# First block of a two-block kernel: another order for the convolution, TensorE's small products, the norm scaling and the rotations

## What is computed

```python
def hybrid_mixer(h, positions, w_in, ...):
    z, xbc, dt_raw, q, k, v, g_ssd, g_att = split_columns(h @ w_in)      # 1024 x 7440
    y_ssd = ssd_mixer(z, xbc, dt_raw, ...) @ w_ssd_out
    q = rope(q, positions); k = rope(k, positions)
    y_att = moba_attention(q, k, v) @ w_attn_out       # 16 heads of 64, causal
    merged = sigmoid(g_ssd) * y_ssd + sigmoid(g_att) * y_att
    return merged @ w_out

def ssd_mixer(z, xbc, dt_raw, ...):
    xbc = silu(causal_dwconv(xbc, conv_w, conv_b))     # 4 taps, 1280 channels
    dt = softplus(dt_raw + dt_bias)                    # 16 heads
    # per chunk of 128 tokens: decay sums of dt*A, decay matrix exp(difference),
    # y_diag = (C B^T * decay) X dt, states, y_off = C states * decay
    y = (y_diag + y_off + X * d_skip) * silu(z)
    return rms_norm per group of 512 columns (y) * norm_w
```

## Time and profile before

| | us |
|---|---|
| three runs | 1402.92, 1403.53, 1398.72 |
| median | 1402.92 |
| span of the profiled execution (the page gives no other time for it) | 1396.5 |
| PE busy | 1319.0 (94%) |
| DVE busy | 841.3 (60%) |
| ACT busy | 727.8 (52%) |
| POOL busy | 600.3 (43%) |

### The profile page before, as it was taken

How to read it: one execution, slowest core, us unless ns; L and a number is a source line. 1 busy time by engine, 2 the same in 40 slices (tenths; PEclk the granted TensorE clock), 3 DMA queues, 4 the chain that set the end, 5 groups by cost and what they waited for, 6 DMA issues and landing times. The chain is left out here.

```text
span 1396.5 us, 22606 instructions
## 1 busy us (share of the span) xinstructions
PE 1319.0 (94%) x7927; PEld 1064.2 (76%) x7927; DVE 841.3 (60%) x1458; ACT 727.8 (52%) x1234; POOL 600.3 (43%) x316
## 2 busy tenths in 40 slices
PE   7989997998899999999889998989999998999997
PEld 6877886776787787878667776767888886788885
DVE  1392436546789888888368899964777763211112
ACT  5555556446476666666564344555433433544443
POOL 5959667440000000000488476836100016687875
PEclk9989998799899999999999999899999999999999
DMA  6736532138599999997475465623100005455562
GB/s 219 204 105 196 154 119 91 61 123 267 177 331 339 322 323 325 328 309 263 143 207 161 135 167 165 187 88 121 62 3 2 17 25 171 153 172 189 170 190 91
DMA packets 128507, 239.97 MB, mean 172 GB/s; under 512 B 16428, under 2 KB 33710, under 8 KB 128420
## 3 DMA queue, kind: packets, MB, share of 16 engines
q1 hardware_dynamic: 116656, 227.12, 51.2%
q10 hardware_dynamic: 11765, 11.67, 3.0%
HBM read 234.57 MB, written 1.05 MB: 169 GB/s over the span
## 5 line engine op out<-in xcount | busy, mean ns | idle before, releaser
L301 POOL TENSOR_TENSOR wlo<-raw,whi 128x1024 fp32r<-128x1024 f32 (+1 forms) x224 | 554.5, 2499 | 623.3 <-ACT whi L296 618.8
L296 ACT ACTIVATE whi<-raw 128x1024 fp32r<-128x1024 f32 (+1 forms) x300 | 308.9, 1053 | 219.9 <-PE bank L325 150.3
L321 PE MATMUL bank<-whi,t0h 128*128 128x512 f32 (+1 forms) x584 | 243.8, 418 | 8.3 <-ACT whi L296 5.7
L322 PE MATMUL bank<-whi,t0l 128*128 128x512 f32 (+1 forms) x584 | 237.2, 406 | 0.0
L325 PE MATMUL bank<-wlo,t0h 128*128 128x512 f32 (+1 forms) x584 | 160.5, 397 | 0.3 <-POOL wlo L301 0.3
L321 PEld LDWEIGHTS bank<-whi,t0h 128*128 128x128 f32 x584 | 115.2, 197 | 41.8 <-ACT whi L296 6.9
L322 PEld LDWEIGHTS bank<-whi,t0l 128*128 128x128 f32 x584 | 115.0, 197 | 25.8 <-issue 1.2
L325 PEld LDWEIGHTS bank<-wlo,t0h 128*128 128x128 f32 x584 | 112.1, 192 | 26.4 <-POOL wlo L301 0.8
L301 DVE TENSOR_TENSOR wlo<-work,whi 128x1024 fp32r<-128x1024 f32 x96 | 113.0, 1219 | 7.8 <-ACT whi L296 7.8
L1605 PE MATMUL bank<-whi,t0h 128*128 128x512 f32 x256 | 106.5, 416 | 0.5 <-issue 0.5
L1606 PE MATMUL bank<-whi,t0l 128*128 128x512 f32 x256 | 101.7, 397 | 0.0
(11 more groups left out here) (521 smaller groups left out, 2486.7 us busy)
## 6 DMA issues: line engine op xcount, KB each, us to landing
raw<-in_w_ff SPq DMA_DIRECT2D x64, 512.0 KB, 3.7
raw<-in_w_in SPq DMA_DIRECT2D x60, 496.0 KB, 3.8
raw<-in_w_in SPq DMA_DIRECT2D x56, 512.0 KB, 3.8
work<-in_w_exp_down SPq DMA_DIRECT2D x68, 256.0 KB, 6.1
work<-in_w_exp_gate SPq DMA_DIRECT2D x62, 256.0 KB, 5.7
work<-in_w_exp_up SPq DMA_DIRECT2D x62, 256.0 KB, 7.4
raw<-in_w_exp_down SPq DMA_DIRECT2D x60, 256.0 KB, 5.9
raw<-in_w_exp_gate SPq DMA_DIRECT2D x34, 256.0 KB, 5.8
```

The source lines that it names most:

```text
L296: nc.scalar.activation(whi[:, s, 0:width], raw_of(n)[:, 0:width], ACT.Copy).then_inc(hi_ready, 1)
L301: ins = (nc.vector if split_by_vector(n) else nc.gpsimd).tensor_tensor(wlo[:, s, 0:width], raw_of(n)[:, 0:width], whi[:, s, 0:width].bitca ...
L321: nc.tensor.matmul(dst[t][:, 0:width], hi[:, k, r], wh[:, kk, :], start=k == 0 and not begun, stop=False)
L322: nc.tensor.matmul(dst[t][:, 0:width], lo[:, k, r], wh[:, kk, :], start=False, stop=False)
```

## The change

- The convolution's sums of the first three taps lie in PSUM (banks 4 to 7, two chunks of 256 columns in each), in groups of eight and two chunks; the fourth tap writes SBUF. It stands behind the first five steps of `dt` instead of ahead of them. `pe_sums_of_decay` waits for the whole convolution, since it writes bank 6.
- PE's table `within` puts the mixer's products behind quarters of a tile instead of behind tiles, and most of them some tiles earlier; ACT's table follows. `pe_sums(q)` comes behind the second quarter of tile 7+q, `pe_diagonal(q)` behind the third of tile 8+q.
- `dve_angles` stands between `xdt_ready` and the wait for `state_done`. The start of y (`begin_y`) stands behind the first `differences`.
- The four norm steps go from DVE to ACT (`act_normed`). y is transposed within tile 14 and split into buffers of its own, `yh` and `yl`.
- `rot` and `rtmp` are doubled. Rotation 1 waits for the last eviction alone, rotation i for the transposes of i-2. POOL's loop is written out; rotation 0 has a semaphore of its own.

```diff
-        y_mean, y_root = sem("y_mean"), sem("y_root")
-        turn_y = Turn(y, gain("ssd_norm_w"), t0h, t0l)
+        y_mean, y_root, y_inverse = sem("y_mean"), sem("y_root"), sem("y_inverse")
+        yh, yl = rounded_over(work_at, "yh", 7680, KC, SEQ), rounded_over(work_at, "yl", 9728, KC, SEQ)
+        turn_y = Turn(y, gain("ssd_norm_w"), yh, yl)
...
-        rot = [carve(2304 + 512 * x, 2, NT, P) for x in range(2)]
-        rtmp = [carve(3328 + 128 * x, NT, 2, 32) for x in range(2)]
+        rot = [[carve(at + 512 * x, 2, NT, P) for x in range(2)] for at in (2304, 11776)]
+        rtmp = [[carve(at + 128 * x, NT, 2, 32) for x in range(2)] for at in (3328, 12800)]
...
-
-
-            between = {3: [pe_xbc], 6: [pe_sums_of_decay, pe_x_back], 7: [pe_cb], 8: [pe_state], 9: [pe_off]}
+                    for part in within.get((p, q), ()):
+                        part(pe)
+                    if q == 1 and SUMS_AT <= p < SUMS_AT + 4:
+                        pe_sums(pe, p - SUMS_AT)
+                    if q == 2 and SUMS_AT < p <= SUMS_AT + 4:
+                        pe_diagonal(pe, p - SUMS_AT - 1)
+
+            within = {(3, 1): [pe_xbc], (5, 2): [pe_sums_of_decay], (5, 3): [pe_x_back], (6, 2): [pe_cb], (7, 0): [pe_state],
+                      (7, 1): [pe_off], (14, 0): [pe_turn_y_first], (14, 1): [pe_turn_y_second]}
             for p in range(IN_T):
                 tile(p)
-                for part in between.get(p, ()):
-                    part(pe)
-                if 9 <= p < 13:
-                    pe_sums(pe, p - 9)
-                if 10 <= p < 14:
-                    pe_diagonal(pe, p - 10)
-            turn_y.pe(pe, [(y_normed, 4)])
             pe.wait_ge(evac_in, NT * IN_T)
...
+        SUMS_AT = 7
+
+        def pe_turn_y_first(pe):
+            turn_y.pe(pe, [(y_normed, 2)], (0, 1))
+
+        def pe_turn_y_second(pe):
+            turn_y.pe(pe, [(y_normed, 4)], (2, 3))
...
-            wide_quarter(pe, Q_SSD + j, j % 4, bank[0:2], t0h, t0l)
+            wide_quarter(pe, Q_SSD + j, j % 4, bank[0:2], yh, yl)
...
-            between = {3: [act_dt_exp], 5: [act_dt_ln, act_conv_silu], 6: [act_z], 7: [act_decays], 8: [act_angles], 13: [act_squares]}
+            between = {2: [act_dt_exp], 3: [act_dt_ln], 4: [act_z, act_conv_silu], 5: [act_decays], 11: [act_angles],
+                       12: [act_squares], 13: [act_normed]}
...
-                if 9 <= p - 1 < 13:
-                    act_lmat(act, p - 10)
+                if SUMS_AT <= p - 1 < SUMS_AT + 4:
+                    act_lmat(act, p - 1 - SUMS_AT)
...
-            pe.wait_ge(xbc_copied, XCH // 2)
+            pe.wait_ge(conv_done, XCH)
...
-            for w in range(4):
...
-                    if w == 0:
-                        order.mark(nc.vector.tensor_scalar(convT[:, c, :], xbcT[:, c, 0:SEQ], tap, None, ALU.mult))
...
-                        ins = nc.vector.scalar_tensor_tensor(out=convT[:, c, :], in0=xbcT[:, c, w:w + SEQ], scalar=tap,
-                                                             in1=convT[:, c, :], op0=ALU.mult, op1=ALU.add)
...
-                order.settle()
             dve.wait_ge(dt_exp, 2)
             order.step(nc.vector.tensor_scalar(s_u, s_exp, 1.0, None, ALU.add))
...
+
+            def partial1(c):
+
+                return bank[4 + c % 8 // 2][:, (c % 2) * SEQ:(c % 2) * SEQ + SEQ]
+
+            for chunks in (range(8), range(8, XCH)):
+                for w in range(4):
+                    for c in chunks:
+                        tap = cwT[:, w * XCH + c:w * XCH + c + 1]
+                        if w == 0:
+                            order.mark(nc.vector.tensor_scalar(partial1(c), xbcT[:, c, 0:SEQ], tap, None, ALU.mult))
+                        else:
+                            ins = nc.vector.scalar_tensor_tensor(out=convT[:, c, :] if w == 3 else partial1(c),
+                                                                 in0=xbcT[:, c, w:w + SEQ], scalar=tap,
+                                                                 in1=partial1(c), op0=ALU.mult, op1=ALU.add)
+                            if w < 3:
+                                order.mark(ins)
+                            else:
+                                ins.then_inc(conv_done, 1)
+                    if w < 3:
+                        order.settle()
+                dve.wait_ge(conv_done, chunks.stop)
...
-            dve_angles(dve, order)
             dve.wait_ge(cum_done, 1)
...
             nc.vector.tensor_tensor(xdtd.rearrange("p (e d) -> p e d", d=DH),
                                     xdt[:, 0, :].rearrange("p (e d) -> p e d", d=DH),
                                     edec.unsqueeze(2).to_broadcast([P, NH, DH]), ALU.mult).then_inc(xdt_ready, 1)
+            dve_angles(dve, order)
             dve.wait_ge(state_done, 1)
             nc.vector.tensor_copy(prevT, bank[7][:, :]).then_inc(state_ready, 1)
-            for t in range(NT):
-                order.mark(nc.vector.tensor_tensor(y[:, t, :].rearrange("p (e d) -> p e d", d=DH),
...
-            order.step(nc.vector.tensor_tensor(y[:, 1, :], y[:, 1, :], xdtd, ALU.add))
+
+            def begin_y():
+
+                for t in range(NT):
+                    order.mark(nc.vector.tensor_tensor(y[:, t, :].rearrange("p (e d) -> p e d", d=DH),
+                                                       xs[:, t, :].rearrange("p (e d) -> p e d", d=DH),
+                                                       dsk.unsqueeze(2).to_broadcast([P, NH, DH]), ALU.mult))
+                dve.wait_ge(off_done, 1)
...
@@ -931,6 +952,8 @@
                 differences(q)
                 if q:
                     add_diagonal(q - 1)
+                else:
+                    begin_y()
...
-            order.step(nc.vector.reciprocal(stat[:, 0:4], stat[:, 0:4]))
-            for t in range(NT):
-                for g in range(2):
-                    o = y[:, t, 512 * g:512 * g + 512]
-                    nc.vector.tensor_scalar(o, o, stat[:, 2 * t + g:2 * t + g + 1], None, ALU.mult).then_inc(y_normed, 1)
+            nc.vector.reciprocal(stat[:, 0:4], stat[:, 0:4]).then_inc(y_inverse, 1)
             turn_y.dve(dve)
-            rotate(dve, nc.vector, order, 0)
+            rotate(dve, nc.vector, order, 0, rot_first, 0)
...
+        def act_normed(act):
+            act.wait_ge(y_inverse, 1)
+            for g in range(2):
+                for t in range(NT):
+                    o = y[:, t, 512 * g:512 * g + 512]
+                    nc.scalar.activation(o, o, ACT.Copy, scale=stat[:, 2 * t + g:2 * t + g + 1]).then_inc(y_normed, 1)
+            turn_y.act(act, 0)
+
         def act_after_in(act):
-            turn_y.act(act, Q_SSD)
...
-        def rotate(eng, ops, order, i):
-
-            if isinstance(i, int) and i == 0:
+        def rotate(eng, ops, order, i, ready, before):
+
+            if i < 2:
                 eng.wait_ge(sin_done, 2)
                 eng.wait_ge(evac_in, NT * IN_T)
+            else:
+                eng.wait_ge(qk_turned, 2 * (i - 1))
...
-            if not (isinstance(i, int) and i == 0):
-                eng.wait_ge(qk_turned, 2 * i)
+            tmp = rtmp[min(i, 1)]
...
-                    dst = rot[x][:, a].rearrange("p t (h a d) -> p t h a d", h=2, a=2)
+                    dst = rot[i % 2][x][:, a].rearrange("p t (h a d) -> p t h a d", h=2, a=2)
...
-                last.then_inc(rot_ready, 1)
-                eng.wait_ge(rot_ready, 2 * i + x + 1)
+                last.then_inc(ready, 1)
+                eng.wait_ge(ready, before + x + 1)
 
         def pool_rotations(pool):
             order = Order(pool, pool_order)
-            with pool.Fori(0, PAIRS // 2 - 1) as i:
-                order.body(0, i, ATT_POOL)
-                rotate(pool, nc.gpsimd, order, i + 1)
-            order.after(0, PAIRS // 2 - 1, ATT_POOL)
+            for i in range(1, PAIRS // 2):
+                rotate(pool, nc.gpsimd, order, i, rot_ready, 2 * (i - 1))
...
-                    pe.wait_ge(rot_ready, 2 * i + x + 1)
+                    if i:
+                        pe.wait_ge(rot_ready, 2 * (i - 1) + x + 1)
+                    else:
+                        pe.wait_ge(rot_first, x + 1)
```

More of the change, by code:

```diff
@@ L843, in dve_ssd @@
             dve.wait_ge(taps_ready, 2)
-            for w in range(4):
-                for c in range(XCH):
-                    tap = cwT[:, w * XCH + c:w * XCH + c + 1]
-                    if w == 0:
-                        order.mark(nc.vector.tensor_scalar(convT[:, c, :], xbcT[:, c, 0:SEQ], tap, None, ALU.mult))
-                    else:
-                        ins = nc.vector.scalar_tensor_tensor(out=convT[:, c, :], in0=xbcT[:, c, w:w + SEQ], scalar=tap,
-                                                             in1=convT[:, c, :], op0=ALU.mult, op1=ALU.add)
-                        if w < 3:
-                            order.mark(ins)
-                        else:
-                            ins.then_inc(conv_done, 1)
```

(1 more changed line is left out.)

30 lines of the change are left out of this document (13 added, 17 removed).

## The result

| | before | changed |
|---|---|---|
| median of 20 runs, us | 1404.42 | 1394.93 |
| lowest, highest | 1397.35, 1409.07 | 1389.34, 1406.19 |
| span of the profiled execution | 1396.5 | 1391.1 |

The ratio is 0.9947 with an interval of 0.9933 to 0.9962: the changed kernel is faster by 5 to 9 us. A second set gave 1398.33 (12 runs) against 1401.34 (23), ratio 0.9971 (0.9946 to 0.9996), 1 to 8 us. The forecast was 1408, slower by 5.

A forecast was written before the change was run, and what follows sets the result against it. TensorE was taken to bound the first block, through five holes and the half clock behind them. Terms 3.4 (up to tile 14) + 9.2 (to the scores) - 7.3 (attention) = +5.3 us on 1402.9 gave 1408, range 1390 to 1420.

The forecast's parts named there:

- The term for attention: Scores to turn of output: GpSimd waits and half clock go, some clock loss returns; 3.5 + 4.6 + 1.6 - 2.4 = -7.3 us.
- the slow stretch around it begins before that hole, so I leave it: Attention, around rotation 3: only the 1.56 us wait for GpSimd goes; the slow clock around it stays.
- the 2.4: Attention's step 0: starting behind a long wait at half clock gives back about half of the 4.6 us won, 2.4.
- 23 x (0.41 + 0.21) = 14.3: Rotation 0 after tile 14: VectorE gets one step per GpSimd step of rotation 1, 14.3 us for 23 steps.
- signs of being wrong: `pe_off` without a wait, rotation 0 under 8 us, or scores under 18 us after tile 14; then time under 1400.
- +9.2: Tile 14 to scores, with turn of y and its wait: 22.4 + 1.9 + 0.6 - 15.7 = +9.2 us.
- the wait for `dA`: Tile 5, after its third quarter: PE waits 2.7 us (0 to 4.5) for `dA`, plus 1.7 of clock (0 to 3.4).
- The wait for `prevT`: Tile 7: angle steps held by GpSimd's subtractions delay `prevT`; PE waits 5.4 us (0 to 8), plus 2.7 of clock.
- the rival of the gaps: Angle steps slip into GpSimd's gaps while rotations alternate; the wait and its clock (8.1 us) go: 1400 us, chance 0.20.
- the one in which VectorE keeps its turns: GpSimd can't get between VectorE's steps, so angles and rotation 0 cost what they do now: -18.6, 1384 us, chance 0.20.
- The third rival, the clock staying down: Half clock lasts longer behind three new waits, through attention's first step: +14, 1417 us, chance 0.26.
- Small products between quarters: 0: Moving `pe_sums` and `pe_diagonal` to other places costs and gains nothing, 0 us.

The follow-up runs named there:

- run with rotation 3 late: Changed kernel in which rotation 3 alone waits for the turn of rotation 2, as before the change; 1398.27 us against 1402.46 before, ratio 0.9980.
- run with GpSimd behind VectorE: Changed kernel, but GpSimd starts rotation 1 only when VectorE has finished rotation 0; 1401.36 us against 1402.46 before, ratio 0.9986.
- two buffers alone: Kernel before with the rotations double-buffered and nothing else; 1391.20 us against 1401.39 before, ratio 0.9929.
- the convolution alone: Kernel before with the convolution's sums in PSUM, in its old place, and nothing else; 1394.92 us against 1401.39 before, ratio 0.9951.
- the run with the angles later: Changed kernel with the 14 angle steps moved in front of the last add_diagonal, the sines one tile later; 1390.13 us against 1402.46 before, ratio 0.9909.
- version with rotation 0 early: Changed kernel with angles later and rotation 0 in VectorE's idle stretches under tiles 12 to 14; 1386.39 against 1401.39 us before, again 1385.60 against 1401.34.

## Why the forecast was wrong

**What failed first: the second slow stretch.** The term for attention was -7.3 and measured -13.9 (-13.4 in the second profile). The step that failed is "the slow stretch around it begins before that hole, so I leave it". By steps: 0 and 1 together became 7.6 us shorter where 5.7 were forecast (3.5 + 4.6 - 2.4; the half clock behind the first scores lasted until 232.7 only, so the 2.4 was nearer 1.2), step 2 became 5.6 shorter where 1.6 was, step 3 0.7 where 0 was: 1.9 + 4.0 + 0.7 = 6.6. The run with rotation 3 late brings 4.8 of step 2's 5.6 us back. The forecast read rightly that the clock fell before the hole, and took from it that the stretch had another cause and would stay. It hung on the late rotation all the same: none of the nine profiles without a late rotation 3 shows the stretch. What joins the late rotation to a fall ahead of its own wait is not shown.

**Second: the price of two alternating streams.** "23 x (0.41 + 0.21) = 14.3" had the right mechanism and the wrong size. It added the time from start to start of each engine working alone; beside each other a pair takes 0.48, and in the changed kernel VectorE got in a step more now and then, 22 steps from 219.84 to 229.23, 0.43 each (first and last here). That makes 9.4 instead of 14.3, 4.9 of the 5.6 us. The rest of that term was right: VectorE's rotation began 2.4 us after tile 14 (forecast 2.3), GpSimd's subtractions ended 6.2 us after it (forecast 6.9). One of the forecast's own signs of being wrong came true by this: scores less than 18 us after tile 14 (16.8), with a time under 1400; and rotation 0 took 13.3 us (215.91 to 229.23), not over 15.

```profile
219.84 0.55 DVE L1082 TENSOR_TENSOR work<-proj,work 128x128 f32<-128x128 f32 x1
...
228.95 0.28 DVE L1085 TENSOR_TENSOR work<-work 128x128 f32<-128x128 f32 x1
```

**Third: two terms that were one.** The sum set "+9.2" for the sharing against "-7.3" for the double buffer, each with bounds of its own. The run with GpSimd behind VectorE shows that they are one trade: what rotation 0 won there (4.7 us), steps 0 and 1 lost to rotation 1 and the clock behind it (5.2).

**What was right.** The part up to the first decay sums: the wait for `dA` was 2.70 (forecast 2.7), the transposes ahead of the convolution came at 52.36 (52.4), the convolution ended at 81 (81.0), its steps took 0.48 to 0.49 us each as recorded, in 16.6 us (forecast 17; before, 31). The clock behind the wait for `dA` cost 1.7 us (half of 82.5 to 85.9; forecast 1.7) in the first profile and 3.4 in the second, the forecast's upper bound. With the sizes of the first profile that part of the sum is -9.1 + 2.7 + 1.7 + 4.2 + 2.5 = +2.0, and the 4.7 of the table less the turn of y (1.9) and its wait (0.8) is +2.0 too; forecast 3.4. The wait for `prevT` was 4.22 (5.4), with the angles held one step per GpSimd subtraction (these began at 102.02, 104.71 and 108.62):

```profile
104.64 0.20 DVE L1045 TENSOR_SCALAR work<-work 128x64 f32<-128x64 f32 x1
104.87 2.21 DVE L1046 TENSOR_SCALAR work<-work 128x64 f32<-128x64 f32 x1
107.12 0.74 DVE L1051 SCALAR_TENSOR_TENSOR work<-work 128x64 f32<-128x64 f32 x3
108.84 2.15 DVE L1057 TENSOR_SCALAR work<-work 128x64 f32<-128x64 f32 x1
```

The wait of 4.22 speaks against the rival of the gaps, the stretched steps against the one in which VectorE keeps its turns. The third rival, the clock staying down, is refuted by the second row of attention: 1.00. "Small products between quarters: 0" was not right, but its error was small and hidden: the earlier sums took away 1.70 us of the hole for the scaling, which the forecast had credited to ScalarE. And the range doesn't follow from the bounds that it names: those of the two waits and their clock give about 1396 to 1417, not 1390 to 1420.

**The parts don't add.** By their ratios two buffers alone give 10 us, the convolution alone 7, and the whole change 7.4 in the first set and 4.1 in the second. About 5.6 go to the angles at their new place (the run with the angles later); what remains, 4 to 7 us, is no more than the intervals of these four figures together allow, and its cause is open.

## What to carry to other kernels

When a change lets VectorE and GpSimd work beside each other on operands in SBUF, price the pair from a row that shows them side by side, and price what the late one would have cost as well: here 4.7 us gained at the start were 5.2 lost in the two steps behind it. A slow stretch that surrounds a wait goes into the sum with the wait, as a whole, unless some execution shows it without, even where the clock falls before the wait. Before giving an engine's small steps a new place, look for one where the next engine isn't waiting: the 14 angle steps cost 5.6 us in one place and nothing some 60 us later.

## What the hardware showed

**A waiting VectorE step can be passed over more than once.** It was seen once. In the run with the convolution alone a 128x32 step with two SBUF inputs began at 51.81, beside a GpSimd subtraction, and ended only when the fourth subtraction in a row had:

```profile
51.81 9.14 DVE L829 SCALAR_TENSOR_TENSOR small<-small 128x32 f32<-128x32 f32 x1
...
47.12 13.78 POOL L301 TENSOR_TENSOR wlo<-raw,whi 128x992 fp32r<-128x992 f32 x6
```

The same step took 2.26 us before, 2.25 in the changed kernel and 0.19 to 2.34 in the other profiles. The Trainium skill (SBUF — State Buffer, Who interferes with whom) says that the one that issues first holds the shared ports for its whole instruction; it doesn't say who is next, and this row shows that it need not be the one that waits.

**The cast is held too.** The forecast left this open between its rows and the Trainium skill. In the changed kernel the cast met an idle GpSimd and took 0.16 us; in the version with rotation 0 early it met a subtraction (GpSimd's order of time has it from 163.35 to 165.95) and took 2.30, to 165.97:

```profile
163.67 2.30 DVE L1040 CAST small<-posi 128x2 f32<-128x2 int32 x1
```

**At small waits the clock is no fixed price.** The version with rotation 0 early was profiled twice. In both, TensorE waited 0.57 to 0.82 us four times between 249 and 263 for ScalarE's exponentials; behind that the clock was half in one execution and full in the other (stretches, columns as above, first and second execution):

```profile
263.80:270.00 6.20, 5.47 (x27) 5.28 (x27) 2.55 (x6) 1.74 (x5) 0.00 (x0) 0.50 0.23 81
```

```profile
263.80:270.00 6.20, 5.18 (x38) 4.54 (x38) 4.71 (x13) 3.13 (x9) 0.00 (x0) 1.00 0.42 143
```

What decides between the two is open. So is what started the fall of the clock at 265.7 before the change: it came behind waits of 0.71 and 0.98 us for ScalarE and ahead of the hole of 1.56, and waits as short were seen with and without a fall.
